# Attention layer of a one-core hybrid diffusion step: another order of the Q, K and V products and of their weight loads

## What is computed

```
mod = (cond_act @ ada_w[i] + ada_b[i])        # ada_w[i]: 1024 x 6144
sh1, sc1, g1, sh2, sc2, g2 = six pieces of mod
h = rms_norm(x, norm1_g[i]) * (1 + sc1) + sh1
```

```
qkv = h @ wqkv                                # wqkv: 1024 x 3072
s_loc = q . k * scale + bias, outside the window -inf
s_ctx = q . ctx_k * scale
p = softmax(concat(s_loc, s_ctx))
o = p_loc . v + p_ctx . ctx_v
m = o @ wo
```

## Time and profile before

| | |
|---|---|
| median of 3 runs | 1356.53 us (1354.65 to 1357.44) |
| the profiled execution | 1354.35 us |
| its span, first to last instruction | 1352.5 us |
| PE busy in the span | 1267.3 us, 94% |
| ring loads (queue q1) | 527.47 MB, 95.6% of the DMA engines' time |
| DMA rate, mean of the span | 396 GB/s |
| attention, first Q product to the end of wo's product | 351.0 to 522.9 us |

### The profile page before, as it was taken

How to read it: one execution, slowest core, us unless ns; L and a number is a source line. 1 busy time by engine, 2 the same in 40 slices (tenths; PEclk the granted TensorE clock), 3 DMA queues, 4 the chain that set the end, 5 groups by cost and what they waited for, 6 DMA issues and landing times.

```text
span 1352.5 us, 18262 instructions
## 1 busy us (share of the span) xinstructions
PE 1267.3 (94%) x6665; PEld 576.3 (43%) x6665; DVE 391.5 (29%) x873; ACT 328.6 (24%) x692; POOL 39.3 (3%) x77
## 2 busy tenths in 40 slices
PE   3877999999999998999999999999999999999996
PEld 0433344343657544443433464443434354434342
DVE  1241222132233314222231413321322443213224
ACT  1231122121322223221221323221212452212122
POOL 3010000000000001000000000000000000000000
PEclk9878999999999999999999999999999999999999
DMA  9999999999997899899999998899999999999995
GB/s 374 419 418 421 420 422 421 423 421 421 343 381 310 324 413 402 340 412 420 421 422 422 418 377 326 339 398 420 422 422 422 415 421 363 405 422 421 421 422 227
DMA packets 87260, 535.21 MB, mean 396 GB/s; under 512 B 11192, under 2 KB 13336, under 8 KB 25760
## 3 DMA queue, kind: packets, MB, share of 16 engines
q1 hardware_dynamic: 82336, 527.47, 95.6%
q0 software_dynamic: 3120, 5.23, 1.2%
q10 hardware_dynamic: 1744, 1.73, 0.4%
HBM read 532.26 MB, written 2.12 MB: 395 GB/s over the span
## 4 chain that ended last, share of the span: by engine, by line
PE 84%; DMA 9%; DVE 4%; ACT 2%; issue 1%; SPq 0%; DVEq 0%; ACTq 0%
PE ps L1869 32%; PE ps L1915 15%; DMA ring<-in_ada_w_dram 5%; PE ps L1855 5%; PE ps L1927 5%; PE ps L1535 4%; PE ps L1499 4%; PE ps L1396 4%; PE ps L1898 3%; PE ps L1544 2%; DMA xh<-in_moe_w_up_dram 2%; DMA ring<-in_attn_wqkv_dram 2%; PE ps L1471 1%; PE ps L1886 1%; PE ps L1705 1%
## 5 line engine op out<-in xcount | busy, mean ns | idle before, releaser
L1869 PE MATMUL ps<-ring,xg 128*64 128x512 f32 x992 | 454.2, 601 | 19.6 <-ACT gu L841 12.3
L1871 PE MATMUL ps<-ring,xg 128*64 128x512 f32 x992 | 451.4, 598 | 0.0
L1869 PEld LDWEIGHTS ps<-ring,xg 128*64 128x64 f32 x992 | 127.6, 137 | 275.2 <-issue 248.2
L1915 PE MATMUL ps<-ring,gb 128*64 128x512 f32 x992 | 225.4, 595 | 0.0
L1319 DVE SCALAR_TENSOR_TENSOR gb<-ps,gslot,g2x 128x512 f32<-128x512 f32 x128 | 90.2, 746 | 257.1 <-PE ps L1915 257.1
L1871 PEld LDWEIGHTS ps<-ring,xg 128*64 128x64 f32 x992 | 126.9, 136 | 0.0
L1915 PEld LDWEIGHTS ps<-ring,gb 128*64 128x64 f32 x992 | 68.4, 137 | 132.2 <-issue 124.6
L854 ACT ACTIVATE y_hi<-gb 128x512 fp32r<-128x512 f32 x128 | 77.1, 626 | 168.3 <-PE ps L1927 108.4
L1396 PE MATMUL ps<-ring,cact 128*32 128x512 f32 x768 | 92.9, 617 | 10.3 <-ACT cact L638 5.3
L841 ACT ACTIVATE gu<-ps 128x512 f32<-128x512 f32 x64 | 38.3, 598 | 231.8 <-PE ps L1871 231.8
L1328 DVE TENSOR_TENSOR y_lo<-gb,y_hi 128x512 fp32r<-128x512 f32 x128 | 83.5, 688 | 12.5 <-ACT y_hi L854 11.9
(11 more groups left out here) (211 smaller groups left out, 1092.8 us busy)
## 6 DMA issues: line engine op xcount, KB each, us to landing
ring<-in_moe_w_up_dram SPq DMA_DIRECT2D x124, 1024.0 KB, 14.8
ring<-in_moe_w_gate_dram SPq DMA_DIRECT2D x124, 1024.0 KB, 13.6
ring<-in_moe_w_down_dram SPq DMA_DIRECT2D x124, 1024.0 KB, 15.4
ring<-in_ada_w_dram SPq DMA_DIRECT2D x96, 1024.0 KB, 17.8
ring<-in_attn_wqkv_dram SPq DMA_DIRECT2D x12, 1024.0 KB, 19.9
spare<-in_moe_w_gate_dram SPq DMA_DIRECT2D x4, 1024.0 KB, 18.8
xh<-in_moe_w_up_dram SPq DMA_DIRECT2D x4, 1024.0 KB, 12.5
hT<-in_moe_w_down_dram SPq DMA_DIRECT2D x4, 1024.0 KB, 13.8
```

Source lines behind the costliest of these rows:

```text
L1869: mg = pe.matmul(ps[0:SLOTS, B_GU, :], xg[:, b, e, :], wg[:, i * F:(i + 1) * F], start=(b == 0), stop=(b == DB - 1))
L1871: mu = pe.matmul(ps[SLOTS:P, B_GU, :], xg[:, b, e, :], wu[:, i * F:(i + 1) * F], start=(b == 0), stop=(b == DB - 1))
L1915: mm = pe.matmul(ps[r * SLOTS:(r + 1) * SLOTS, DOWN_BANKS[e % 2], :], acts[:, e % ACTS, j, :], w[:, i * D + r * HALF:i * D + (r + 1) * HAL ...
```

## The change

The order of the units in `BEFORE_EXPERTS[1]` becomes

```diff
@@ BEFORE_EXPERTS, layer 1
-    ada_units(4)[:4] + matrix_units("qkv", 0) + matrix_units("qkv", 2) + ada_units(4)[4:]
-    + matrix_units("qkv", 4) + ada_units(5) + matrix_units("qkv", 1) + matrix_units("qkv", 3) + ada_units(6)
+    ada_units(4)[:4] + matrix_units("qkv", 0) + ada_units(4)[4:] + matrix_units("qkv", 1)
+    + matrix_units("qkv", 2) + matrix_units("qkv", 4) + ada_units(5) + matrix_units("qkv", 3) + ada_units(6)
@@ jobs and banks
-        Q0, K0, FLIPS, CK_TURNS, K_TURN0, V0, Q1A, K1A, Q1B, K1B, V1A, K_TURN1, V1B = 0, 2, 4, 8, 10, 11, 13, 14, 15, 16, 17, 18, 19
-        JOBS = "adad" + "dddd" + "aaa" + "ad" + "adad" + "aad"
-        JOB_BANK = [0, 4, 5, 6, 7, 0, 4, 5, 6, 7, 0] + [4, 5] * 4 + [4]
+        Q0, Q1A, Q1B, K0, FLIPS, CK_TURNS, K_TURN0, V0, K1A, K1B, V1A, K_TURN1, V1B = 0, 2, 3, 4, 6, 10, 12, 13, 15, 16, 17, 18, 19
+        JOBS = "adadad" + "dddd" + "aaa" + "ad" + "ad" + "aad"
+        JOB_BANK = [0, 4, 5, 6, 7, 0] + [4, 5, 6, 7] + [0, 4, 5] + [4, 5] * 3 + [4]
@@ ACT, attention
                 empty(Q0, blocks(qT, 0, 2))
+                empty(Q1A, blocks(qT, 4, 2))
                 empty(K0, blocks(kT, 0, 2))
...
                 exps(2)
-                empty(Q1A, blocks(qT, 4, 2))
 
                 copy_turned(2)
                 exps(3)
+                empty(K1A, blocks(kT, 4, 2))
 
                 copy_turned(3)
                 exps(4)
-                empty(Q1B, blocks(qT, 6, 2))
@@ DVE, attention
                 empty(Q0 + 1, blocks(qT, 2, 2))
+                empty(Q1B, blocks(qT, 6, 2))
                 empty(K0 + 1, blocks(kT, 2, 2))
...
                 bias_max(2)
+                normalise(2)
                 ada_rows(5, l, base)
                 copy_output(0)
-                normalise(2)
...
                 normalise(3)
-                empty(K1A, blocks(kT, 4, 2))
...
                 normalise(4)
+                empty(K1B, blocks(kT, 6, 2))
...
                 normalise(5)
-                empty(K1B, blocks(kT, 6, 2))
@@ PE, attention
                 by_channel(Q0 + 1, w, 1)
+                ada(4, 4, ADA_UNITS, l, base)
+                w = weights(1)
+                by_channel(Q1A, w, 0)
+                by_channel(Q1B, w, 1)
                 w = weights(2)
                 by_channel(K0, w, 0)
                 by_channel(K0 + 1, w, 1)
...
                 turned(K_TURN0, [kT[:, i, 0:SEQ] for i in range(4)])
-                ada(4, 4, ADA_UNITS, l, base)
-
+
+                emptied(FLIPS + 2)
+                emptied(FLIPS + 3)
                 emptied(CK_TURNS)
                 emptied(CK_TURNS + 1)
                 scores(0)
...
                 ada_turn(4)
-                emptied(K_TURN0)
                 turn(0)
                 scores(1)
                 by_token(V0 + 1, w, 1)
-                ada(5, 0, 4, l, base)
+                ada(5, 0, 2, l, base)
 
                 turn(1)
                 scores(2)
-                ada(5, 4, ADA_UNITS, l, base)
+                ada(5, 2, ADA_UNITS, l, base)
                 emptied(V0)
                 emptied(V0 + 1)
                 attend(0)
-                w, wk = weights(1), weights(3)
-                by_channel(Q1A, w, 0)
-
-                ada_turn(5)
+
                 turn(2)
                 scores(3)
+                ada_turn(5)
                 attend(1)
-                by_channel(K1A, wk, 0)
+                w = weights(3)
+                by_channel(K1A, w, 0)
 
                 turn(3)
-                emptied(Q1A)
                 emptied(K1A)
                 scores(4)
                 attend(2)
-                by_channel(Q1B, w, 1)
+                by_channel(K1B, w, 1)
+                ada(6, 0, 2, l, base)
 
                 turn(4)
                 scores(5)
                 attend(3)
-                by_channel(K1B, wk, 1)
-                ada(6, 0, 4, l, base)
+                ada(6, 2, ADA_UNITS, l, base)
 
                 turn(5)
-                emptied(Q1B)
                 emptied(K1B)
                 scores(6)
-                ada(6, 4, ADA_UNITS, l, base)
```

## The result

The changed kernel took 1364.55 us (median of 4 runs, 1362.39 to 1365.80), the kernel before beside it on the same chip 1355.74 us (1354.65 to 1357.44). The ratio is 1.006, 95% interval 1.0045 to 1.0075: **slower by about 8 us** (8.1 by the ratio, 8.8 by the two medians), as forecast (+8.0, 1364.5). The profiled execution after, the shortest of its four runs, took 1362.39 us, with a span of 1360.4 us against 1352.5.

A forecast was written before the change was run, and what follows sets the result against it. Loads bound most of the kernel, PE bounds attention, where its losses reach the end. Stall 6.2 + clock 1.5 + first scores 0.3 = +8.0 us, giving 1364.5 us against the median 1356.53; range 1358.5 to 1368.5.

The forecast's parts named there:

- What bounds the kernel: Loads at their rate through most of the span; in attention PE alone, with under 0.2 us in 42 to give.
- The stall: Start of attention: PE waits 6.2 us (bounds 2.1 to 6.7) for units 9 and 11, ahead of Q's third product; chance 0.83.
- The part in the adaLN units: Second half of ada 4: 1.7 us of PE's wait, its last unit landing at 369.3.
- the price of the bias rows: Start of attention: the four bias-row loads cost the ring 8.2 us while units 6 to 11 load.
- The clock: First matmuls of Q1A, behind the wait: slower clock costs +1.5 us, bounds 0 to 5.1.
- The first scores: scores(0), after K's transposes: waits for ACT's copies of the cached keys, no longer hidden by ada 4; +0.3 us.
- The softmax's cover: Pairs 2 and 5: less PE work hides the softmax, but it fits with 1.4 us over; cost 0.
- The rival on the cover: Softmax of pairs 2 and 5 comes out 2 us longer, making PE wait; 1365.7 us or more, chance 0.03.
- The rival of the bias rows giving way: Start of attention: the ring gets 88%, unit 11 lands at 368.3, no wait for loads; +0.3, 1356.8 us, chance 0.10.
- The loads deciding: Hole in the loads from 413 to 455: up to 15.3 us comes back, so faster, 1341.2 us; chance 0.04.

The follow-up runs named there:

- the doubled cost: Four extra, unread loads of the same bias rows: added to the base 1373.15 us, ratio 1.0121; added to the kernel before 1367.11 us, ratio 1.0081.
- the base: The changed kernel with the bias rows laid out in two blocks in SBUF, same pieces; 1364.48 us, ratio 1.0062 against the kernel before.

## Why the prediction was right

**What bounds the kernel.** Right for most of attention, and that a loss on PE there reaches the end was shown by the doubled cost (9.1 us in attention, 7.9 to 8.7 between the medians). Too coarse in one point: I read the hole of 413 to 455 as "the ring is full" for all of attention behind its start. Up to 412.5 the ring of the kernel before was still just in time, and its loads landed 2.5 us apart until 433.2; only then did they stop. This did not enter the sum, but it made me expect the wrong thing of the kernel before with the cost doubled.

**The stall.** Taken at 6.2 us, measured 5.4 (0.75 us of waiting ahead of the last adaLN unit, 4.46 ahead of Q1A, and 0.2 that the trace does not show as a wait). The landings carried it: unit 11 forecast at 374.7, landed at 373.73, in an execution that began attention 0.2 us sooner. The part in the adaLN units was put too high, 1.7 us for 0.75, since unit 9 landed at 368.3 instead of 369.3. What was a little off is the price of the bias rows: 373.7 - 350.7 - 15.6 = 7.4 us here, for 8.2 in the one execution that it was read from. That the bias rows cause it, put at 8.2 us of the ring's time, is shown by both sides: unit 11 lands 7 us sooner when they come later, and 8.4 us later when they come twice.

**The clock.** Taken at 1.5 us from one row of 16 transposes; the four products took 29.38 - 27.86 = 1.5 us more, at a granted 0.51 for 3.5 us. That the clock was the cause is shown by the run with PE kept at work, where it stayed at 1.00 and the loss was gone. The size is no constant, and that it came out the same is luck: 2.4 us in the base's profile. The Trainium skill's page "TensorE: Matmul & The Clock Gate", section "HAM oscillation — how this bites in real kernels", says that a kernel whose matmuls wait long enough for loads is put back to half clock and starts its next matmuls cold. The trace agrees: 0.51 behind the wait of 4.46 us.

**The first scores.** Taken at 0.3 us, measured 0.39, and 0 where an adaLN half stands in between again.

**The softmax's cover.** Taken at 0: PE has no idle time in the pairs (41.97 of 42.00 us and 45.00 of 45.00 busy), and the adaLN units put back left attention at 171.8 us with the changed pairs in it. The rival on the cover is out.

**The rival of the bias rows giving way.** Half of it came true. Between 354 and 358 the queues of the kernel after read

```profile
q1 hardware_dynamic: 103, 0.72, 80.3%
q0 software_dynamic: 102, 0.35, 27.7%
```

The ring's share rose from 48.9% to 80.3%, its pieces now the long ones of adaLN units, one for one with those of the bias rows (103 to 102 packets). The Trainium skill's page "DMA: Bandwidth & Descriptors", section "Queues, rings and completion order", says that an engine takes turns between queues packet by packet; the counts agree. So unit 7 landed at 358.6 instead of 363.3. But the bias rows were through at 351.3 + 16.6 = 367.9, ahead of unit 11 in both kernels, and the ring had lost its 7.4 us to them by then. Only the last unit's landing counted.

**The loads deciding.** Out: the hole stayed, at 252 GB/s, and the kernel got slower. It moved, as forecast: before, no ring load landed between 433.2 and 445.8, and now none does between 410.9 and 430.4.

The sum was 8.0: 6.2 + 1.5 + 0.3. Measured in attention 7.5: 5.4 + 1.5 + 0.4 and 0.2 that I can't assign. Attention began 0.2 us sooner and ended 7.3 later, and the span grew by 7.9; the other 0.6 us lie behind attention and were not followed up. The agreement of the median with the forecast to 0.05 us is luck: the runs of one kernel scatter by 3 us, and the kernel before, run beside it, came out 0.8 us below the median that the forecast starts from.

## What to carry to other kernels

Moving work forward in a program also moves forward the moment at which its data are asked for: list the landing of each unit beside the time at which the new order asks for it, and the difference is the price. Do it for every unit up to the next place where the queue is surely ahead, not for the first alone, since a loss of the queue costs whatever exceeds the smallest margin behind it. A small load on another queue can be the dearest of all if it runs where the ring is empty; here it cost nothing measurable when it ran 17 us later.

## What was not expected of the hardware

1 MB of bias rows in pieces of 256 bytes (64 float32) cost the ring between 5.6 us (loaded later) and 9.8 us (the second set in the kernel before), where 1 MB of adaLN weights takes 2.5. No run here tells whether that is the pieces or the queue by which they come.

And the granted clock does not answer the same wait with the same loss. Behind 4.46 us of waiting it was at its lower level for 3.5 us in the changed kernel's profile; behind 4.44 us in the base's, from 372.3 to 379.0, so that it fell 1.9 us before the products began. The products ran at that level for 3.1 and 4.8 us and lost half of it, 1.5 and 2.4 us. These are single executions.

```profile
370.00:380.00 10.00, 5.82 (x16) 4.76 (x17) 0.00 (x0) 0.00 (x0) 0.00 (x0) 0.66 1.05 387
372.30:379.00 6.70, 4.82 (x11) 3.87 (x12) 0.00 (x0) 0.00 (x0) 0.00 (x0) 0.50 1.05 387
```
